# A float32 transformer kernel: the memory's key and value projection cut into 16 pieces and placed inside the second mixer

## The reference

```python
x = x + y @ w_out[l]                               # y: retention and RWKV-7 mixers side by side
x = x + memory_cross_attention(rmsnorm_2(x, norm_xattn[l]), rmsnorm_2(mem, norm_mem[l]),
                               xattn_w_q[l], xattn_w_kv[l], xattn_w_o[l])
# inside: q = h @ w_q ;  k, v = split(mem_n @ w_kv)      mem: 256 x 1024, w_kv: 1024 x 2048
```

## Time and profile before

| | us |
|---|---|
| median of 3 runs (lowest, highest) | 2814.22 (2813.64, 2818.51) |
| the profiled execution's own time | 2819.79 |
| span of its trace | 2817.8 |
| PE, DVE, ACT busy in it | 2567.3, 1859.6, 1307.7 |
| mean granted TensorE clock | 0.961 |

### The profile page before, as it was taken

The page is one execution under the profiler, slowest core; times in us unless marked ns, Lnnn a source line. Parts: engine busy times, 40 slices in busy tenths (PEclk is TensorE's granted clock), DMA queues, the critical chain, the costliest instruction groups (busy, mean ns, idle before and its releaser), DMA issues. The chain is left out here.

```text
span 2817.8 us, 45777 instructions
## 1 busy us (share of the span) xinstructions
PE 2567.3 (91%) x17160; PEld 2309.7 (82%) x17160; DVE 1859.6 (66%) x3769; ACT 1307.7 (46%) x1964; POOL 498.5 (18%) x320
## 2 busy tenths in 40 slices
PE   5698999999999999689999999999999779897989
PEld 4588999997888888389999997888879468686978
DVE  6676999858777764555888757666664464544654
ACT  3345654555454453444665555555554210354343
POOL 0001666721000001000666721000000200000000
PEclk9899999999999999799999999999999898999999
DMA  8655777753777746144767643666645100242544
GB/s 344 255 172 156 211 217 221 219 171 84 265 259 265 265 163 225 43 143 141 185 181 184 182 134 91 218 217 217 218 145 185 69 1 1 75 161 78 173 135 155
DMA packets 200506, 480.68 MB, mean 171 GB/s; under 512 B 54448, under 2 KB 87728, under 8 KB 199760
## 3 DMA queue, kind: packets, MB, share of 16 engines
q1 hardware_dynamic: 150960, 432.01, 45.5%
q10 hardware_dynamic: 12576, 47.29, 4.4%
q0 software_dynamic: 36864, 0.15, 3.3%
HBM read 461.41 MB, written 17.96 MB: 170 GB/s over the span
## 5 line engine op out<-in xcount | busy, mean ns | idle before, releaser
L271 DVE TENSOR_TENSOR weight_low<-weight_raw,weight_high 128x1024 fp32r<-128x1024 f32 x732 | 893.0, 1222 | 429.6 <-ACT weight_high L265 424.5
L399 PE MATMUL bank<-h_high,weight_high 128*128 128x256 f32 x3552 | 1022.7, 288 | 84.5 <-DVE weight_low L271 24.8
L265 ACT ACTIVATE weight_high<-weight_raw 128x1024 fp32r<-128x1024 f32 x732 | 773.8, 1059 | 670.0 <-DMA weight_raw<-peer_v_dram 343.7
L399 PE MATMUL bank<-h_low,weight_high 128*128 128x256 f32 x3552 | 1017.3, 286 | 0.0
L399 PE MATMUL bank<-h_high,weight_low 128*128 128x256 f32 x3552 | 1016.7, 286 | 0.0
L399 PEld LDWEIGHTS bank<-h_high,weight_high 128*128 128x128 f32 x3552 | 693.8, 195 | 102.1 <-issue 84.0
L399 PEld LDWEIGHTS bank<-h_low,weight_high 128*128 128x128 f32 x3552 | 694.0, 195 | 0.0
L399 PEld LDWEIGHTS bank<-h_high,weight_low 128*128 128x128 f32 x3552 | 693.5, 195 | 0.0
L1091 POOL DMA_INDIRECT gate_table<-pick_expo,pick_spot x256 | 457.9, 1789 | 772.4 <-DVE pick_expo L1193 466.9
L1367 PE MATMUL bank<-weight_high,act_high 128*128 128x512 f32 x1024 | 318.5, 393 | 6.7 <-DVE act_low L1420 6.1
L1367 PE MATMUL bank<-weight_low,act_high 128*128 128x512 f32 x1024 | 316.9, 391 | 0.0
(11 more groups left out here) (327 smaller groups left out, 2532.9 us busy)
## 6 DMA issues: line engine op xcount, KB each, us to landing
weight_raw<-peer_u_dram SPq DMA_DIRECT2D x256, 512.0 KB
weight_raw<-peer_v_dram SPq DMA_DIRECT2D x256, 512.0 KB
later_modulations<-ada_later_dram ACTq DMA_DIRECT2D x54, 512.0 KB, 4.4
gate_table<-later_modulations ACTq DMA_DIRECT2D x8, 2048.0 KB, 16.7
weight_raw<-peer_w_q_dram SPq DMA_DIRECT2D x32, 512.0 KB
gate_tiles<-gate_table SPq DMA_DIRECT2D x256, 64.0 KB, 3.3
weight_raw<-w_in_dram SPq DMA_DIRECT2D x32, 512.0 KB
weight_raw<-mlp_w_up_dram SPq DMA_DIRECT2D x32, 512.0 KB
```

Of the source, the lines that this page charges most:

```text
L265: self.nc.scalar.activation(self.high[:, slot, :], self.raw[:, slot, :], ACT.Identity) \
L271: eng.tensor_tensor(self.low[:, slot, :], self.raw[:, slot, :], self.high[:, slot, :].bitcast(F32), ALU.subtract) \
L399: mm = self.nc.tensor.matmul(out, w, x, start=(start and i == 0), stop=(stop and i == 2), skip_group_check=skip)
```

## The change

The 16 tiles of `w_kv` move from a projection of their own into 13 blocks of `retention` and `rwkv`, mostly where `keep_warm` stood. The segment order becomes `w_in_2, xattn_w_kv, w_out_2, xattn_w_q`. The norm of `mem` moves too: its load and its eight squares go into the second layer's expert loop, its scaling and splitting beside the `w_in_2` tiles. Results go to a buffer `kept` of 4096 columns, which shares its space with `silu`, `later`, `gates` and `pick.sums`, all of them done with by then. `MemoryProjection` holds the pieces:

```diff
+class MemoryProjection:
+    def load(self, sp, *tiles):
+        for n in tiles:
+            if n + RING < self.seg.count:
+                self.core.load_tile(sp, self.seg, n + RING, n % RING)
+            else:
+                self.core.load_tile(sp, self.following, n + RING - self.seg.count, n % RING)
+    def multiply(self, pe, *tiles):
+        for n in tiles:
+            core.wait_turn(pe, self.seg, n // RING, n % RING)
+            if n >= 2:
+                pe.wait_ge(self.kept.sem, self.kept.at(n - 1))
+            for c in range(KB):
+                mm = core.product(self.bank(n), n % RING, (core.mem_high[:, c, :], core.mem_low[:, c, :]), c, c == 0, c == KB - 1)
+            mm.then_inc(self.used.sem, 1)
+    def keep(self, act, *tiles):
+        for n in tiles:
+            act.wait_ge(self.used.sem, self.seg.first + RING + n + 1)
+            core.nc.scalar.activation(core.kv[:, n, :], self.bank(n), ACT.Identity).then_inc(self.kept.sem, 1)
```

```diff
 def block_rms(...)
-            core.keep_warm(banks + 1, bank=3)
+            if memory is None:
+                core.keep_warm(banks + 1, bank=3)
+            else:
+                memory.multiply(pe, *tiles)
 def second_mixer(core):
     second_projection(core)
-    retention(core)
-    rwkv(core)
+    memory = MemoryProjection(core)
+    retention(core, memory)
+    rwkv(core, memory)
     core.split(view(core.arena, 20736, 8, T), core.h_high, core.h_low)
-    core.linear("vector", core.add_to_x(), loads=[(view(core.arena, 2048, 8, T), "mem")], squares=core.x, root=core.work[:, 0:T])
+    core.linear("vector", core.add_to_x(), squares=core.x, root=core.work[:, 0:T])
 def cross_attention(core):
-    core.linear("scalar", core.copy_to(q), norm=plain_norm(core, "norm_xattn_2"), squares=mem, root=mem_root)
-    core.linear("scalar", core.copy_to(kv), norm=(mem, core.col("norm_mem_2"), None, mem_root))
+    core.linear("scalar", core.copy_to(q), norm=plain_norm(core, "norm_xattn_2"))
     token_major(core, [(kv[:, 8:16], tokens)])
```

More of the change, by code:

```diff
@@ L1377, in _ @@
                     tile(turn, slot)
+            if not beside:
+                pe.wait_ge(mem_added.sem, KB - 1)
+                nc.tensor.matmul(core.bank[0][:, 0:T], core.c("ones"), mem_total, start=True, stop=True).then_inc(mem_summed.sem, 1)
             for slot in range(RING):
@@ L1474, in _ @@
                     .then_inc(swapped.sem, 1)
-            core.keep_warm(2)
+            if memory is None:
+                core.keep_warm(2)
+            else:
+                memory.multiply(pe, 0)
+        if memory is not None:
+            @block.sync
+            def _(sp):
+                memory.load(sp, 0)
+            @block.scalar
+            def _(act):
+                memory.high(act, 3)
+                memory.keep(act, 0)
         if clearing:
@@ L1504, in rope, with block_rms @@
         s.close(pairs)
-def block_rms(core, src, blocks, ones, count, eps, squares, root, centre=None):
+def block_rms(core, src, blocks, ones, count, eps, squares, root, centre=None, memory=None, tiles=(), highs=(), lows=()):
     nc, sig = core.nc, core.sig
@@ L1525, in _ @@
                     .then_inc(summed.sem, 1)
-            core.keep_warm(banks + 1, bank=3)
+            if memory is None:
+                core.keep_warm(banks + 1, bank=3)
+            else:
+                memory.multiply(pe, *tiles)
+        if memory is not None:
+            @block.sync
+            def _(sp):
+                memory.load(sp, *tiles)
         @block.scalar
@@ L1530, in _ @@
             core.prepare_root()
+            if memory is not None:
+                memory.high(act, *highs)
             for n in range(banks):
@@ L1537, in _ @@
             nc.scalar.activation(root_f, root_f, ACT.Exp, scale=-0.5)
+            if memory is not None:
+                memory.keep(act, *tiles)
         @block.vector
@@ L1552, in _ @@
             step.used = link.n
+            if memory is not None:
+                memory.low(dve, *lows)
     step.close(step.used)
@@ L1955, in _ @@
             core.prepare_root()
+            memory.high(act, 9)
             for i in range(2):
@@ L2204, in rwkv @@
     centred, squares, root = area(0), area(1), area(2)
-    block_rms(core, y, 4, "half_ones", 64, core.c("eps_rwkv"), squares, root, centre=centred)
+    block_rms(core, y, 4, "half_ones", 64, core.c("eps_rwkv"), squares, root, centre=centred, memory=memory, tiles=(12, 13),
+              lows=(15,))
     with nc.Block() as block:
@@ L2212, in _ @@
             mm.then_inc(full.sem, 1)
-            core.keep_warm(5)
+            memory.multiply(pe, 14, 15)
+        @block.sync
+        def _(sp):
+            memory.load(sp, 14, 15)
+        @block.scalar
+        def _(act):
+            memory.keep(act, 14, 15)
         @block.vector
```

159 lines of the change are left out of this document (136 added, 23 removed).

## The result

The changed kernel took **2766.03 us** (median of 4 executions, 2760.92 to 2769.40) beside 2813.93 for the kernel before (4 executions): a ratio of 0.9836, with a 95% interval of 0.9813 to 0.9858. Two later comparisons gave 0.9846 [0.9826, 0.9866] and 0.9836 [0.9812, 0.9860]. The forecast was 2773 us, range 2761 to 2787, faster.

A forecast was written before the change was run, and what follows sets the result against it. Each block was bound by its longest engine list. Removing 53.2 us less 11.8 coming back gained 41.4: 2819.8 profiled became 2778.4, and 5.6 lower for the median gave 2773 us, range 2761 to 2787.

The forecast's parts named there:

- bounds on the costs: All blocks taking tiles: returned costs of 8 to 17 us, giving 2769 to 2778 us.
- What goes: Between the last copies of w_q and w_kv: 53.2 us removed, 45.9 of products and 7.3 around them.
- rival E: Removed stretch hid a second bound, so the change doesn't do what it says: 2814 us, chance 0.01.
- What comes back: Costs in the blocks that take the moved work, summed block by block: 11.75 us.
- Expert loop: Second layer's expert loop: one added matmul with ones on PE costs 0.45 us.
- Rope: Rope block: half clock behind PE's new 3.3 us idle would add 1.8; half taken, +0.9 us.
- Heads: Memory attention's heads: tiles 1 and 2 fill PE's wait and keep the clock full, -0.5 us, bounds -1.3 and +2.4.
- Key norm: Key norm block: ACT's last copy waits behind a load and high half, +1.0 us, between 0 and 2.
- rival A: Mixer full of real products keeps clock up; 8 us half-clock stretch in first inversion tile rare: 2765 us, chance 0.17.
- B: Tiles run at half clock because restarts behind barriers stay slow: 2792 us, chance 0.07.
- C: Chain of slot, load, high and low halves runs late in the mixer: +9, 2782 us, chance 0.15.
- D: Inversions: without the 12 zeros the clock stays at half, +74 us, 2847 us, chance 0.02.

The follow-up runs named there:

- B: The kernel before, without the change: 2813.93 us (median of 4 executions) beside the changed kernel's first measurement.
- A: The changed kernel, against the kernel before: 2766.03 us, ratio 0.9836.
- all parts: A with third tile's halves out of w_in_2, two tiles in inversion gaps, highs 10 and 11 in decays, five zeros behind inversion products: 2770.17 us, ratio 0.9838.

## Why the prediction was right, step by step

The range held and so did the way of summing; the forecast figure itself was 7 us too high. It was built on three executions of B, of 2813.64 to 2818.51 us, where the median of 46 later ones is 2808.5. And the profile of B, from which the stages were read, has the stretch.

One sum in the prediction is wrong. Its bounds on the costs, "8 to 17", don't follow from the terms named there: 11.75 - 0.9 - 0.8 - 1.0 is 9.05, and 11.75 + 0.9 + 2.9 + 1.0 + 1 + 1 is 18.55. That gives 2770 to 2780, and the result lies below it; it lies within the range by the 8 us of the clock alone.

**What goes: right.** The stretch of 53.2 us is missing, and nothing stood in its place; rival E is out. Two small gains were not in the sum: `w_q` is 0.83 shorter, and of that 0.65 came with the squares of `mem` moved alone (28.95 to 28.30); and the `token_major` ahead of the inversions is 0.80 shorter, which no run isolates.

**What comes back: 11.75 forecast.** In the table the terms of the mixer and its ends make 2.43 + 1.00 + 0.21 + 0.79 + 0.72 + 0.71 + 2.55 + 3.67 + 1.70 = 13.8, and 0.5 in `w_out_2`. Seven of the eleven terms were right within 0.2 us, and where I moved them away they went: the third tile's halves carry 2.4 and 0.97, tiles 12 and 13 carry 2.87 and 1.72.

*Expert loop*, 0.45: not told apart from what differs there between executions (the last copy of `w_in_2` begins anywhere from 2182.5 to 2191.2 us over all the traces).

*Rope*, 0.9, taken as half of 1.8: the mechanism was right (half clock behind the idle). Its size was that of the matmuls, 1.66, of which DVE's slack took 0.66. The Trainium skill, which I weighed there ("TensorE: Matmul & The Clock Gate", Part 1: The HAM clock gate), has the throttled state as the default, released by activity. From it I took that every restart behind the idle is slow. For this one the trace agrees: 5.33 us for eight matmuls. For the restart behind the 1.04 us of idle it doesn't in A; in B half clock came, but 2 us behind the restart.

*Heads*, -0.5, in fact +0.21: a step that failed. I held that tiles 1 and 2 keep the clock up through the mixing, above 0.9 for the stage. They do until 2214.8, and behind the 3.55 us of idle that remain the matmuls go to half clock again, 0.84 over the stage. Three zeros in that idle gave 19.57, which is my bound of -1.3 (20.98 - 1.3 = 19.7). The mask's load, which DVE awaits, was 0.33 later in the block.

*Key norm*, 1.0, in fact 2.55 (2.56 in the repeat): mis-sized by more than its bound of 2. The chain is the one that I wrote, used 7, load, high 11, keep 8; but the block begins at half clock. Its sums took 3.78 us instead of 2.57, tile 6 was 0.9 late as well, so each step behind stood some 2 us later. Moving highs 10 and 11 took 1.64 of it away.

**The clock in the inversions.** I gave rival A 0.17 and put 8.0 us on it. In all three profiles of A, and in those of three variants of it (three idles filled, third tile moved, two tiles in the gaps), the stretch is absent; in both of B, in that with the norm alone moved, and with highs 10 and 11 moved, it is there. The kernels differ from the last `w_in_2` copy on. From there to the end B took 628.1 and 628.0 us, A 579.8 and 580.0: 48.3 and 48.0 less. Without the 8.0 of the stretch that is 40.3 and 40.0, where the terms of this part sum to 53.2 - 11.3 = 41.9. So the sum was right to 2 us, and in the profiles rival A's 8 us come on top.

How often B has the stretch is not shown. Its 46 executions reach from 2801.87 to 2824.77, 25 up to 2809.36 and 21 from 2811.63 on, with mean clocks of 0.962 to 0.966 and of 0.959 to 0.964; the 14 of A reach from 2760.92 to 2770.22. Less time at half clock in the lower group fits a stretch that some executions lack, but both profiles of B are of the upper group. What lies ahead of the mixer differs by up to 8.7 us between traces too. By medians of all 46 and all 14, 2808.5 and 2765.8, A gains 42.8, near the forecast 41.4. If B's are a mixture of executions with and without the stretch, this agreement owes something to luck.

Whether A avoids the stretch for a cause, or by where its idles fall in time, stays open: A, B and the moved highs have the same idle of 1.04 us ahead of it. Rival A's reason, a mixer full of real products, is not enough: the kernel with the highs moved has the same products and has the stretch. The stretch goes with what came before it. Leaving out B without its zeros (7.67, half clock in three pieces), and where nothing fills that idle, the `token_major` ahead of the inversions took 8.5 to 8.7 us in the four traces that have the stretch, and 7.55 to 8.0 in the six that don't. The two go together; no run tests whether one causes the other. With the idle filled the stretch was absent in three profiles of three (B, highs moved, all parts), of kernels that had it or would have had it by their `token_major` (8.6 to 8.75). That supports the idle as a condition, and it is not sufficient.

**The other rivals.** B: no tile behind a barrier ran at half clock in the last two blocks; tile 6 did. C: loads land 3.4 us behind their issue (2257.91 to 2261.33), as in the earlier trace rows; what was late in the key norm came mostly from the clock. D: a clock of 0.93 over the inversions without any zeros in the mixer.

## What to carry to other kernels

Work that only fills waits costs what its last piece adds behind the block's longest list, and this could be summed here block by block to 2 us. Look first at handovers: the halves of a tile that nobody needs yet, behind the last copy, left PE idle for 3.24 us at one place, which cost 2.4, and for 3.56 at another. Then compare executions with the clock of the stage in hand: a gain of 1 to 3 us in a block that restarts at half clock may be given back in another block, or a third may gain as well, and only the trace shows it. Sum to the end of the program, and not to the end of the part that you changed.

## What the runs showed of the hardware that I had not expected

The granted clock of a stage can change with things far ahead of it. With two high halves moved out of the key norm, a stretch at half clock that cost 8 us began some 66 us later; it is in the one profile of that kernel and in none of A's three. Filling three idles, or removing one, left the mixer's mean clock where it was, 0.94: the half clock turned up in the low-rank block (13.7 instead of 12.2 us) and the last `block_rms` (12.95 instead of 11.60), and in both it was gone from `w_q` (26.9 and 26.65 instead of 28.15).

In each inversion tile the 24 matmuls of one tile of `w_kv`, in eight steps, took the places of two zeros matmuls and of five idles of 0.48 us, and the inversions didn't grow: 109.38 against 109.69.

A matmul of float32 zeros of 512 columns holds PE for 0.89 us at full clock, two records each, where a split-form matmul of 256 columns takes 0.12.
